# Attention of a two-block network: order of scores, mixing, maxima and weight conversion, and the keys' copies in two transfers

## The reference, cut to what matters

```
q, k, v = split(h @ w_in, 3)                 # 16 heads of 64
s = einsum('bqhd,bkhd->bhqk', qb, kb) * scale + bias
p = softmax(where(valid, s, -inf))
o = einsum('bhqk,bkhd->bqhd', p, vb)         # per 64-position chunk, own chunk and 8 before it
return o @ w_out
```

## Time and profile before

| | us |
|---|---|
| median of 3 runs | 1962.59 (1961.82 to 1962.74) |
| the profiled execution, its own time | 1963.07 |
| its span, first to last instruction | 1961.3 |
| TensorE busy | 1902.0 (97%) |
| VectorE busy | 1082.8 (55%) |
| GpSimd busy | 792.8 (40%) |
| ScalarE busy | 681.0 (35%) |
| mean granted TensorE clock | 0.993 |

### The profile page before, as it was taken

The page is one execution under the profiler, slowest core; times in us unless marked ns, Lnnn a source line. Parts: engine busy times, 40 slices in busy tenths (PEclk is TensorE's granted clock), DMA queues, the critical chain, the costliest instruction groups (busy, mean ns, idle before and its releaser), DMA issues.

```text
span 1961.3 us, 22406 instructions
## 1 busy us (share of the span) xinstructions
PE 1902.0 (97%) x8716; PEld 1574.8 (80%) x8716; DVE 1082.8 (55%) x1471; ACT 681.0 (35%) x976; POOL 792.8 (40%) x325
## 2 busy tenths in 40 slices
PE   7998999999999999999999999999999999999997
PEld 5776888888878888888888888888888888888886
DVE  5897872663685544343572625364777665435263
ACT  4224432222363333332432322234656542222232
POOL 4332444444453343333344444443223244444441
PEclk9999999999999999999999999999999999999998
DMA  5311332443232222222243323233233222323231
GB/s 164 99 65 63 120 101 93 142 137 101 77 102 86 77 75 86 86 86 86 65 127 89 104 91 103 92 100 111 76 106 101 76 86 87 107 88 106 88 105 43
DMA packets 163495, 186.31 MB, mean 95 GB/s; under 512 B 4016, under 2 KB 143552, under 8 KB 163280
## 3 DMA queue, kind: packets, MB, share of 16 engines
q1 hardware_dynamic: 154512, 169.36, 26.8%
q10 hardware_dynamic: 8896, 15.75, 2.8%
HBM read 178.76 MB, written 6.33 MB: 94 GB/s over the span
## 4 chain that ended last, share of the span: by engine, by line
issue 47%; PE 22%; POOL 22%; DVE 4%; ACT 3%; POOLq 0%; DMA 0%; ACTq 0%; DVEq 0%; SPq 0%
POOL w_lo L383 22%; PE ps L394 7%; PE ps L396 7%; PE ps L395 7%; DVE probs_t_lo L1624 1%; ACT w_hi L774 1%; DVE q_lo L1595 1%; DMA x<-in_x_dram 0%; ACT work L1035 0%; DVE work L1618 0%; DVE work L1224 0%; ACT work L1050 0%; DVE q_hi L1595 0%; ACTq L1014 0%; DVE work L1605 0%
## 5 line engine op out<-in xcount | busy, mean ns | idle before, releaser
L383 POOL TENSOR_TENSOR w_lo<-raw,w_hi 128x1024 fp32r<-128x1024 f32 x320 | 792.4, 2480 | 1135.4 <-ACT w_hi L774 1135.4
L774 ACT ACTIVATE w_hi<-raw 128x1024 fp32r<-128x1024 f32 x320 | 336.4, 1058 | 748.6 <-PE ps L396 747.1
L394 PE MATMUL ps<-xh,w_hi 128*128 128x512 f32 x1408 | 556.9, 396 | 16.6 <-DVE xl L1156 15.6
L396 PE MATMUL ps<-xh,w_lo 128*128 128x512 f32 x1408 | 549.7, 390 | 0.0
L395 PE MATMUL ps<-xl,w_hi 128*128 128x512 f32 x1408 | 549.5, 390 | 0.0
L394 PE MATMUL ps<-hid_hi,w_hi 128*128 128x512 f32 x944 | 370.3, 392 | 11.2 <-issue 7.3
L395 PE MATMUL ps<-hid_lo,w_hi 128*128 128x512 f32 x944 | 368.3, 390 | 0.0
L396 PE MATMUL ps<-hid_hi,w_lo 128*128 128x512 f32 x944 | 368.1, 390 | 0.0
L394 PEld LDWEIGHTS ps<-xh,w_hi 128*128 128x128 f32 x1408 | 265.3, 188 | 75.7 <-issue 14.5
L395 PEld LDWEIGHTS ps<-xl,w_hi 128*128 128x128 f32 x1408 | 265.4, 189 | 56.2 <-issue 2.4
L396 PEld LDWEIGHTS ps<-xh,w_lo 128*128 128x128 f32 x1408 | 265.2, 188 | 55.7
(11 more groups left out here) (179 smaller groups left out, 1563.4 us busy)
## 6 DMA issues: line engine op xcount, KB each, us to landing
raw<-in_mlp_w_dram SPq DMA_DIRECT2D x64, 1024.0 KB, 5.3
raw<-in_ret_w_in_dram SPq DMA_DIRECT2D x24, 1024.0 KB, 5.1
raw<-in_att_w_in_dram SPq DMA_DIRECT2D x12, 1024.0 KB, 5.4
raw<-in_w_gate_dram SPq DMA_DIRECT2D x11, 1024.0 KB, 5.3
raw<-in_w_up_dram SPq DMA_DIRECT2D x11, 1024.0 KB, 5.3
raw<-in_w_in_dram SPq DMA_DIRECT2D x10, 1024.0 KB, 5.1
raw<-in_w_down_dram SPq DMA_DIRECT2D x8, 1024.0 KB, 5.2
raw<-in_ret_w_out_dram SPq DMA_DIRECT2D x8, 1024.0 KB, 5.1
```

The lines of the kernel that those rows point to most:

```text
L383: nc.gpsimd.tensor_tensor(view[0], view[1], view[2].bitcast(F32), ALU.subtract).then_inc(w_lo, c.made(w_lo))
L394: nc.tensor.matmul(o, a[0], b[0], start=first, stop=False, skip_group_check=True)
L396: return nc.tensor.matmul(o, a[1], b[0], start=False, stop=last, skip_group_check=True)
L774: nc.scalar.activation(view[0], view[1], ACT.Copy).then_inc(w_hi, c.made(w_hi))
```

## The change

Four things, in the attention only:

- TensorE: where a group opens, `scores(h + 1)` stand ahead of `mix(h - 1)`. In the last group, from s == 2 on, the output unit stands ahead of the scores.
- VectorE: `maxima` stand ahead of the low part of the keys (and of `mixed_add` and `value_lo`) where a group opens; at the start, `maxima(1)` stand ahead of the second `value_lo`. In the last group `out_narrow` stands ahead of the maxima from s == 2 on.
- ScalarE: at the start, the two half blocks behind unit 2 (one of them the second half of the value weights) are converted ahead of the high parts of unit 1 (keys). In the last group, from s == 2 on, the exponentials stand behind the conversion and the copy of the mixed head.
- `k_hi` and `k_lo` become one tensor `k_parts`, so that `copy_k` moves high and low part together: two transfers of 256 KB in place of four of 128 KB.

```diff
-        kh = sb("k_hi", [P, 2, SEQ], F32R)
-        kl = sb("k_lo", [P, 2, SEQ], F32R)
+        k_parts = sb("k_parts", [P, 4, SEQ], F32R)
+        kh, kl = k_parts[:, 0:2, :], k_parts[:, 2:4, :]
...
                             unit_v(X)
+                            scores(h + 1)
                             mix(h - 1)
-                            scores(h + 1)
                             turn(h)
...
-                        if last_group:
+                        if last_group and s == 1:
+                            scores(h + 1)
+                            pe.wait_ge(mix_ready, 8)
+                            unit4_narrow(s - 1)
+                        else:
+                            if last_group:
+                                unit4_narrow(s - 1)
+                            else:
+                                qk_unit(s - 1)
                             if h + 1 < ATT_HEADS:
                                 scores(h + 1)
...
-                        for a, b in ((kh[0:64, t, :], kh[64:P, t, :]), (kl[0:64, t, :], kl[64:P, t, :]),
-                                     (ko[64:P, t, :], ko[0:64, t, :]), (ko[64:P, 2 + t, :], ko[0:64, 2 + t, :])):
+                        both = slice(t, t + 3, 2)
+                        for a, b in ((k_parts[0:64, both, :], k_parts[64:P, both, :]), (ko[64:P, both, :], ko[0:64, both, :])):
                             act.dma_start(b.bitcast(F32), a.bitcast(F32)).then_inc(k_copied[t], 16)
...
                     qk_hi(0, 1)
-                    qk_hi(1)
                     c.of[qk_ready].n = qk_before_att
-                    for n in (2, 3):
-                        qk_done(n)
-                        if n == 3:
-                            copy_k(0)
-                        qk_hi(n)
+                    qk_done(2)
+                    qk_hi(1, 1)
+                    qk_hi(2)
+                    qk_done(3)
+                    copy_k(0)
+                    qk_hi(3)
...
                     normalise(0)
+                    maxima(1)
                     value_lo()
-                    maxima(1)
                     normalise(1)
...
                             qk_taken(3)
+                            maxima(h + 1)
                             qk_lo(3)
                             mixed_add(h - 1)
                             value_lo()
-                            maxima(h + 1)
                             normalise(h + 1)
```

More of the change, by code:

```diff
@@ L652, in scores @@
                             pe.wait_ge(qk_ready, c.next(qk_ready, 2))
-                            pe.wait_ge(k_copied[h % 4 // 2], 64 * (h // 4 + 1))
+                            pe.wait_ge(k_copied[h % 4 // 2], 32 * (h // 4 + 1))
                         t = h % 4 // 2
@@ L1086, in _ @@
                             v_unit(1)
-                        if last_group:
-                            if h + 1 < ATT_HEADS:
-                                exps(h + 1)
+                        if last_group and s == 1:
+                            exps(h + 1)
                             after_unit()
@@ L1092, in _ @@
                         else:
-                            qk_unit(s - 1)
+                            if last_group:
+                                after_unit()
+                            else:
+                                qk_unit(s - 1)
                             mixed_copy(h - 1)
-                            exps(h + 1)
-                            if s == 2:
+                            if h + 1 < ATT_HEADS:
+                                exps(h + 1)
+                            if s == 2 and not last_group:
                                 copy_k(0)
@@ L1672, in _ @@
                             value_lo()
-                        if last_group:
+                        if last_group and s == 1:
+                            maxima(h + 1)
+                            normalise(h + 1)
+                            out_narrow(s - 1)
+                            mixed_add(h - 1)
+                        elif last_group:
+                            out_narrow(s - 1)
                             if h + 1 < ATT_HEADS:
                                 maxima(h + 1)
+                            mixed_add(h - 1)
+                            if h + 1 < ATT_HEADS:
                                 normalise(h + 1)
-                            out_narrow(s - 1)
-                            mixed_add(h - 1)
                         else:
```

## The result

| | us |
|---|---|
| before, median (5 runs beside the changed kernel) | 1961.82 (1960.69 to 1962.74) |
| changed, median of 5 runs | 1950.99 (1949.28 to 1952.92) |
| ratio, 95% interval | 0.9946 (0.9936 to 0.9957) |
| changed, profiled execution: own time, span | 1950.77, 1949.0 |
| mean granted TensorE clock | 0.994 |

The change is faster by 10.8 us (0.54%). The forecast was 1950.5 us, a gain of 12.05 us from a median of 1962.59.

What follows compares the result with a forecast made beforehand. TensorE was taken as the bound, with attention idle time and low-clock matmul time to win: 7.3 + 3.1 - 0.35 - 0.45 + 0 + 1.2 + 1.25 = 12.05 us, giving 1950.5 us; range 1945.3 to 1956.0.

Steps and rivals of the forecast that it cites:

- Openings, 7.3 us: Three group openings: the turn's wait of 2.44 us for the next head's maxima goes each time, 7.3 us won.
- Clock behind the openings, 3.1 us: Value units behind two openings: the low clock goes with the idle time, 2 x 1.57 = 3.1 us won; bounds 0 and 3.1.
- the expectation for open_both: Openings' order alone: waits of 7.5 us and low clock of 3.1 us go, 10.6 us faster; its rival said 7.5.
- The start, a loss of 0.45 us: First value unit waits for VectorE, held by GpSimd, and starts 0.6 us later; 0.45 us lost.
- the low clock stays: At the start: TensorE idles longer, so the clock stays low, some of it passing while idle; unit ends 0.45 us later.
- The bound of 1.5 us for the clock: Start's best case: value unit starts at 1357.9 at full clock, 1.5 + 1.6 + 0 = 3.1 us won.
- Keys' copies, 1.2 us won: Three waits for the keys' copies: two larger transfers save 0.4 us each, 1.2 us won; bounds 0 and 2.85.
- the prediction's estimate of 2.4 us: Keys' copies: 512 KB over 64 partitions need 2.4 us at half of the full rate, making that term 0.9 us.
- h = 12, 0.35 us lost: Opening at h = 12: output unit wants the second value unit's low part at once; 0.35 us lost, bounds 0 and 1.
- Head 0, nothing: Head 0's turn: earlier maxima(1) bring TensorE 1.2 us of 1.4, none counted since VectorE paces the next two heads.
- Last group, 1.25 us: Last group: the 0.9 us wait in the scores of head 15 and its restart go, 1.25 us won; bounds 0 and 1.25.
- TensorE needs them at 3.35: Last group: maxima end 3.1 to 3.3 us after the output unit, and TensorE needs them at 2.55 + 0.8 = 3.35.

Runs made afterwards that it cites:

- the halves: Kernel before with TensorE's half of the openings' order alone, 1966.67 us (1.0016 to 1.0036), and with VectorE's half alone, 1955.99 us (0.9965 to 0.9984).
- open_both: Kernel before with the openings' new order alone, on TensorE and VectorE, at h = 4, 8, 12; 1955.02 us, ratio to before 0.9955 to 0.9980.
- four_copies: Changed kernel with the keys' copies in four transfers again; 1951.81 us, ratio to before 0.9931 to 0.9958.
- start_act: Kernel before with ScalarE's new order at the start alone; 1964.47 us, ratio to before 1.0005 to 1.0023.
- two_copies: Kernel before with the keys' copies in two transfers alone; 1958.36 us, ratio to before 0.9979 to 0.9998.
- split_convert: Changed kernel with one half block converted behind unit 2 and two behind unit 3, in place of two and one; 1950.11 us, ratio to before 0.9928 to 0.9955.

## Why the prediction was right, and where it was not

Of the signs that the prediction named for being right, four hold: no turn at h = 4, 8 and 12 waits, the value units there take 5.83 us, the start waits for VectorE, and one low part of keys takes over 2 us. The fifth, a low clock at the start, doesn't.

- **Openings, 7.3 us.** Measured 7.45, and the halves show the mechanism: the maxima were behind steps that wait for the mixing. That GpSimd would hold the negated maxima until its end held in open_both and four_copies, not in the changed kernel; it cost nothing at the turn either way.
- **Clock behind the openings, 3.1 us.** 1.5 us at h = 5 and 1.5 at h = 13: right, and no wait over 1.3 us is left there. But the expectation for open_both carried it over to a kernel in which a new wait of 2.38 us appeared.
- **The start, a loss of 0.45 us.** The chain was right to 0.2 us: which low part is held, for how long, when the value unit starts (0.73 us later than before). The step that failed is "the low clock stays": it stayed in start_act and four_copies (25.48 us from the column sums to the scores), not in the changed kernel (24.00), so 0.79 us were won there. That is luck of the profiled execution: the wait of the start was no good ground for either answer (below). The bound of 1.5 us for the clock also left out who waits next: with the old start a clock that stayed up brought only 0.2 to 0.5 us, since the scores then waited for the copies.
- **Keys' copies, 1.2 us won.** Wrong in sign: 0.76 us lost. The step that failed is that the wait was priced by the rate at which the bytes move. They did move faster, at the end faster (270 to 295 GB/s) than the half rate that the prediction's estimate of 2.4 us took as the limit, and were over sooner; but the landing came 0.8 us after them in place of 0.3. What the two transfers do bring, 1.1 us of ScalarE, I had named and not priced: 0.51 us in the steps behind (3.6 us from scores to key unit in two_copies too, 3.8 in four_copies), and the end of GpSimd's hold on the negated maxima at each opening.
- **h = 12, 0.35 us lost.** Measured 0.63, by another wait: scores of head 14 wait for the keys' copies, issued late (1519.11) and landing beside a weight block, 1.29 us. Before, these copies had landed 1.5 us ahead of the scores; the full clock of the value unit ahead of them (1.5 us) used that up. Against it stands a wait of 0.73 us of the output unit for values, which the kernel before had at this place and the prediction's list of idle time lacks: it is gone. I had looked only at who waits for values.
- **Head 0, nothing.** 0.03 us; right, for the reason given.
- **Last group, 1.25 us.** 1.13 won, 0.28 given back at the mixing of head 14, whose low parts of probabilities now follow the later normalisation. I had that margin at "TensorE needs them at 3.35" for the maxima only.

With signs: 7.45 + 3.0 + 0.8 - 0.25 - 0.63 + 0.85 = 11.2 us. The errors of the two worst steps, 1.2 us at the start (too pessimistic) and 1.4 us at the copies (too optimistic), cancelled.

## What to carry to other kernels

Where one engine feeds the bound one, put what the bound engine waits for ahead of everything that in its turn waits for a third engine, and then ask who wanted the deferred steps; here the copies did. Price a saved issue by what is queued behind it on the issuing engine, and a transfer by its landing, not by its last bytes. And judge changes of some us by waits in the trace: behind equal waits, low-clock stretches of 1.5 us each came in one trace and not in the next.

## What the runs showed of the hardware

VectorE and GpSimd. Instructions on VectorE that normally take 0.69 us or 0.17 us took 2.75 us and up to 2.31 us when GpSimd's 2.4 us instruction was at work, and ended within about 0.7 us of GpSimd's end; with GpSimd's second half away (split_convert) the low part of keys was short again. The Trainium skill, SBUF — State Buffer, section on who interferes with whom, has this as an exclusive port pair held for a whole instruction; the runs agree. A shift of 1.2 us in GpSimd's start made the negated maxima at the openings 1.5 us or 0.3 us long (four_copies, changed).

Copies. The same 512 KB within SBUF moved at 193 GB/s as four transfers (before, 1399.66 to 1402.16), and as two at 210 GB/s, with 270 to 295 GB/s in the last 1 us (changed, 1398.52 to 1399.52), and still landed 0.25 us later.

The clock. In the attention of the thirteen traces, the granted clock fell to the lower level (a value unit behind then took 7.1 to 7.4 us in place of 5.8) after these waits of TensorE: 1.82 to 1.84 us at the start, 2 of 7 times; 2.55 us there, 2 of 3; 1.98 us at an opening, 1 of 3; 2.23 to 2.27 us, 7 of 12; 3.28 us, 3 of 3; of the single waits of 2.38, 2.81 and 3.05 us in the last group, after the first only. After waits of up to 1.65 us it never fell there. So in this kernel's attention a wait of about 2 us costs its length and, roughly every second time, up to 1.5 us more; what decides in the single case stays open.
